# Attention scores issued two head pairs ahead, together with moved modulation sums and split waits, in a two-block transformer kernel

## The reference, cut to what matters

```
first block, DEPTH = 2 layers:
  h = x @ w_in[l]                       # 1024 x 5024, split into latents, gates, q, k, v
  o_a = softmax attention, 8 heads of 96/64 (latents up-projected, rotary on 32 channels)
  o_b = differential attention, 4 heads of 2 x 64
  x = layer_norm(alpha * x + merged(o_a, o_b, gates) @ w_out)

second block, DEPTH = 2 layers:
  mod = silu(c) @ mod_w[i] + mod_b[i]   # 1024 x 9216: shift, scale and gate of three sublayers
  x = half ffn; (layer 0 also: ctx = half ffn)
  layer 0: window attention, 16 query heads, 4 key heads of 64, over 256 banded latent
           keys + 256 context keys + a sink logit per head
  layer 1: fourier mix:  real(fft over tokens of fft over channels, 4 groups of 256) @ fourier_wo
  x = post_norm; x = half ffn
```

## Time and profile before

| | us |
|---|---|
| runs | 1606.33, 1601.07, 1602.33 |
| median | 1602.33 |
| the profiled execution | 1607.04 |
| its span, first to last instruction | 1605.3 |
| TensorE busy in it | 1560.0 (97%) |
| VectorE busy | 1201.6 (75%) |
| ScalarE busy | 795.2 (50%) |
| mean granted TensorE clock | 0.994 |

### The profile page before, as it was taken

One profiled execution on the slowest core, in us unless ns is written; L12 is line 12 of the kernel. 1 busy time (PEld: TensorE's weight loads), 2 busy tenths in 40 slices (PEclk: granted clock), 3 DMA queues, 4 the chain that ended last, 5 costly groups with the idle time before them and its releaser, 6 DMA issues.

```text
span 1605.3 us, 20700 instructions
## 1 busy us (share of the span) xinstructions
PE 1560.0 (97%) x7671; PEld 1289.4 (80%) x7671; DVE 1201.6 (75%) x1853; ACT 795.2 (50%) x1250; POOL 153.7 (10%) x212
## 2 busy tenths in 40 slices
PE   7999998999999999999999899999999999999997
PEld 6888886888788887888877568888888888888886
DVE  7888996898988785877759767877587776575554
ACT  5476543566454453544535656444354443264442
POOL 1100001100011110011100121111011110010000
PEclk9999998999999999999999999999999999999999
DMA  9864558754678876788756217888678874365552
GB/s 343 271 236 146 185 166 288 247 176 143 209 255 271 284 259 216 235 275 278 257 174 207 76 53 254 283 276 277 199 237 277 281 269 164 93 222 184 184 186 77
DMA packets 200652, 349.62 MB, mean 218 GB/s; under 512 B 11204, under 2 KB 128252, under 8 KB 200044
## 3 DMA queue, kind: packets, MB, share of 16 engines
q1 hardware_dynamic: 174812, 252.90, 47.9%
q0 software_dynamic: 25744, 95.43, 16.9%
HBM read 347.21 MB, written 1.08 MB: 217 GB/s over the span
## 4 chain that ended last, share of the span: by engine, by line
PE 84%; DVE 12%; DMA 2%; ACT 1%; issue 1%; SPq 0%; DVEq 0%; POOLq 0%; ACTq 0%
PE acc L618 25%; PE acc L620 24%; PE acc L619 24%; DVE w_lo L1606 2%; PE turn L1008 1%; PE acc L915 1%; PE score L767 1%; DMA mod_raw<-in_mod_w 1%; PE score L895 1%; DVE att_work L2231 1%; DVE acc_ctx L1726 1%; PE score L1106 1%; PE turn L904 1%; DVE wide L1988 1%; PE score L959 1%
## 5 line engine op out<-in xcount | busy, mean ns | idle before, releaser
L1606 DVE TENSOR_TENSOR w_lo<-raw,w_hi 128x1024 fp32r<-128x1024 f32 (+2 forms) x490 | 585.4, 1204 | 245.0 <-ACT w_hi L1222 244.4
L1222 ACT ACTIVATE w_hi<-raw 128x1024 fp32r<-128x1024 f32 (+2 forms) x490 | 502.1, 1039 | 455.9 <-PE acc L620 438.0
L618 PE MATMUL acc<-w_hi,xT_hi 128*128 128x512 f32 (+1 forms) x1440 | 572.1, 397 | 3.5 <-DVE xT_lo L1654 2.1
L620 PE MATMUL acc<-w_hi,xT_lo 128*128 128x512 f32 (+1 forms) x1440 | 561.5, 390 | 0.0
L619 PE MATMUL acc<-w_lo,xT_hi 128*128 128x512 f32 (+1 forms) x1440 | 560.7, 389 | 0.0
L618 PEld LDWEIGHTS acc<-w_hi,xT_hi 128*128 128x128 f32 x1440 | 271.6, 189 | 59.2 <-issue 6.3
L620 PEld LDWEIGHTS acc<-w_hi,xT_lo 128*128 128x128 f32 x1440 | 271.1, 188 | 56.7
L619 PEld LDWEIGHTS acc<-w_lo,xT_hi 128*128 128x128 f32 x1440 | 271.7, 189 | 52.6
L506 POOL DMA_DIRECT2D mod_raw<-in_mod_w x144 | 104.3, 724 | 909.0 <-DVE mod_run L1726 745.4
L618 PE MATMUL acc<-w_hi,hT_hi 128*128 128x512 f32 x440 | 172.8, 393 | 0.0
L620 PE MATMUL acc<-w_hi,hT_lo 128*128 128x512 f32 x440 | 171.4, 390 | 0.0
(11 more groups left out here) (295 smaller groups left out, 1303.6 us busy)
## 6 DMA issues: line engine op xcount, KB each, us to landing
raw<-in_ffn_wi SPq DMA_DIRECT2D x220, 512.0 KB, 5.0
mod_raw<-in_mod_w POOLq DMA_DIRECT2D x144, 512.0 KB, 6.1
raw<-in_ffn_wo SPq DMA_DIRECT2D x110, 512.0 KB, 4.5
raw<-in_w_in SPq DMA_DIRECT2D x72, 512.0 KB, 6.1
raw<-in_w_out SPq DMA_DIRECT2D x16, 512.0 KB, 4.6
raw<-in_attn_wqkv SPq DMA_DIRECT2D x16, 512.0 KB, 4.6
wide<-in_b_merge POOLq DMA_DIRECT2D x4, 1024.0 KB, 9.2
raw<-in_w_branch_a SPq DMA_DIRECT2D x8, 512.0 KB, 4.6
```

What stands on the lines that cost most here:

```text
L618: nc.tensor.matmul(dst, xh, wh, start=start, stop=False)
L620: return nc.tensor.matmul(dst, xl, wh, start=False, stop=stop)
L1222: nc.scalar.activation(piece_part(w_hi[:, i % SPLIT_SLOTS, :], i), piece_part(raw[:, s, i % 2 * PIECE:(i % 2 + 1) * PIECE], i), ACT.Copy). ...
L1606: nc.vector.tensor_tensor(piece_part(w_lo[:, i % RAW_PIECES, :], i), piece_part(raw[:, i // 2 % RAW_SLOTS, i % 2 * PIECE:(i % 2 + 1) * PIE ...
```

## The change

- The second and third modulation sum of layer 1 of the first block go behind the steps n = 1 and n = 3 instead of n = 0 and n = 2. Layer 0 is as it was.
- In the window attention TensorE waits for a new signal, `heads_rotated`, before it turns q, and for the copied keys only before the keys. One of VectorE's splits goes from behind the copy of the keys to the last head pair.
- `scores(u + 2)` is issued inside `turn_probs(u)`: token tile 0 of both heads before the fourth group of turns, token tile 1 behind that group and before the inverse sums. `scores(1)` stays where it was.
- In the fourier stage tile 1 is turned and modulated one group later, behind g = 3 of tile 0 and that group's move and split; the wait for all four banks becomes one wait for each group.

```diff
+        heads_rotated = sem("heads_rotated")
...
                     project(ACC[n % 2 * 2:n % 2 * 2 + 2], 4)
-                    if n % 2 == 0:
+                    if n % 2 == l:
                         mod_sum(True)
...
-                pe.wait_ge(k_twice_ready, 1)
+                pe.wait_ge(heads_rotated, 1)
                 for u in range(4):
                     pairs(u, lambda t, i: qkv[:, t, (2 * u + i) * P:(2 * u + i) * P + P])
...
-                def scores(u):
-                    for t in range(NT):
+                def scores(u, tiles=range(NT)):
+                    for t in tiles:
...
                     for i in range(2):
                         pe.wait_ge(exps_ready, c.next("exps"))
                         for t in range(NT):
+                            if i and t and u + 2 < AH // 2:
+                                scores(u + 2, (0,))
                             b = att_turn(u, 2 * i + t)
...
+                    if u + 2 < AH // 2:
+                        scores(u + 2, (1,))
                     pe.wait_ge(inv_ready, c.next("inv", 2))
...
                 for u in range(AH // 2):
-                    if u + 1 < AH // 2:
-                        scores(u + 1)
+                    if u == 0:
+                        scores(1)
                     if u:
                         values(u - 1)
                     turn_probs(u)
...
-                        if t == 0 and g == FGROUPS - 1:
+                        if t == 1 and g == 0:
                             after.append(turn_tile(1))
...
-                landed(*ACC)
 
                 after = []
                 for g in range(FGROUPS):
+                    landed(ACC[g])
                     b = turn_bank(g)
...
-                    step(nc.vector.tensor_tensor(xs, r0, r1, ALU.add))
+                    return nc.vector.tensor_tensor(xs, r0, r1, ALU.add)
...
-                        rotate_heads(0, 0, AH)
+                        step(rotate_heads(0, 0, AH))
...
-                        rotate_heads(1, 0, AH)
+                        rotate_heads(1, 0, AH).then_inc(heads_rotated, 1)
+                        dve.wait_ge(heads_rotated, 1)
...
-                    rotate_heads(t, AH, ROPED)
+                    step(rotate_heads(t, AH, ROPED))
...
                 m.then_inc(k_twice_ready, 1)
-                split()
...
                     else:
-                        split(2)
+                        split(3)
...
                     for g in range(FGROUPS):
-                        if t == 0 and g == 2:
+                        if t == 1 and g == 0:
                             modulate_tile(1)
```

## The result

Over six runs of each kernel the changed one takes 1607.89 us (median, 1606.53 to 1612.55), the kernel before 1602.55 (1600.56 to 1606.33). The ratio is **1.0032**, 95% interval 1.0020 to 1.0044: some 5 us slower. The forecast was 1603.8, a loss of 1.5, in a range of 1598.0 to 1608.5. The measured time lies in the range, the loss is over three times the forecast one, and it stands on the border of 0.3%, past which "slower" had 0.12.

The account below looks back on a forecast made before the run. TensorE was taken to bound the kernel (busy 97% of the span). Layer 1 +0.7, attention +0.6 and fourier +0.2 sum to +1.5 us on the median 1602.33, giving 1603.8, range 1598.0 to 1608.5.

Parts of the forecast that it names:

- Layer 1's mechanism: Layer 1: the 6.73 us stall isn't removed but goes to pieces 13 and 14, the latter bound by feature 0's load.
- the term +0.3 + 0.4: Layer 1's moved sums: +0.3 us for the stall moving to pieces 13 and 14, +0.4 for the clock.
- I take half, +0.4: Layer 1: half of the 0.9 us loss if the clock returns only after 7.2 us of work, slowing pieces 14 and 15.
- the clock rival: Layer 1: pieces 14, 15 and the second sum run at 1.2 GHz; +8.2 us in total, 1610.5; chance 0.09.
- +0.3: Layer 1: with the second sum moved, it ends at 284.16 against 283.89 before, leaving out the clock.
- The weight load: Layer 1: taken as 0; its rival has SP's weight load delay feature 0, piece 14 3.5 us later: 1607.3, chance 0.07.
- Start of the attention: Attention start: the split taken out brings the first maxima earlier, −0.9 us, between −1.2 and 0.
- the limit named: Attention start: the mask lands at 887.66, while the removed split would bring the first maxima to 887.42.
- The scores: Attention loop: first half fills waits (−0.96, −2.2), values 0 to 5 wait for ScalarE (+4.1): +0.9 us, period 7.17.
- the tail: Attention, last pair: the third split delays the move before the fourth turn by 0 to 1.17 us; +0.6 taken.
- The rival in which ScalarE's move is hidden: Attention: the 4.1 us of waits before values 0 to 5 don't come; −2.6 us in total, 1599.7; chance 0.12.
- Fourier: Fourier stage: tile 1 modulated behind group 3, four groups end at 1370.1 against 1369.94, +0.2 us; bounds −1.7 and +1.2.

Follow-up runs that it names:

- bias_loads_later: The changed kernel with GpSimd's merge-bias and norm-row loads (3 MB) issued one chunk of features later: 1602.16 us, 0.9987 of the kernel before.
- sums_only: The kernel before with only the layer-1 sums moved: 1608.4 us, ratio 1.0028.
- kept_busy_sized: The changed kernel with unread products filling TensorE's waits: 14 before piece 13, 24 before piece 14, 9 before fourier tile 1; 1607.31 us, 1.0019 of the kernel before.
- attention_only: The kernel before with only the attention part of the change: 1605.19 us, ratio 1.0010.
- late_half: The changed kernel with the second half of the scores behind the inverse sums instead of in front: 1605.45 us, 1.0009 of the kernel before.
- fourier_only: The kernel before with only the fourier part of the change: 1604.01 us, ratio 1.0000.
- late_half_bias_later_sums: The kernel before with the attention part, scores' second half behind the inverse sums, bias loads one chunk later and layer-1 sums moved: 1599.93 us, 0.9969.
- attention_late_half: The kernel before with the attention part alone, the second half of the scores behind the inverse sums: 1601.19 us, 0.9980.
- late_half_bias_later: The kernel before with the attention part, scores' second half behind the inverse sums, and bias loads one chunk later: 1599.43 us, 0.9974.
- before_bias_later: The kernel before with GpSimd's merge-bias and norm-row loads issued one chunk later: 1602.97 us, 0.9988.

## Why the prediction was right and wrong

- **Layer 1's mechanism was right.** The stall moved to pieces 13 and 14 and the second part is bound by feature 0's load: the waits are 3.45 and 4.48 us, where 5.10 and up to 5.5 were written. bias_loads_later shows the cause: with the load early the second wait is gone. The fall of the clock was read slightly late, too: 0.84 in the window 264 to 265 puts it at 264.7, 3.7 us after TensorE stopped and not 3.9, which changes nothing in the sum.
- **Its size was wrong: the term +0.3 + 0.4 measured 3.1 in the two profiles and 4.5 in the runs of sums_only.** The step that failed is "I take half, +0.4". It carried the clock's loss over from one fall, piece 13's, and asked if the level would be back in time. It was back (0.90 and 0.95 in the windows from 272 to 276). But behind the next gap, which the forecast had at up to 5.5 us, it was down again, with piece 14 on the path and in two of the three a part of piece 15, in all three unfilled traces with the sum moved; kept_busy_sized puts this at 2.4 us. It is in part what the clock rival said (pieces 14, 15 and the sum at 1.2 GHz), but by another way: the level came back and fell again, it rose within piece 15, and the whole lost 5.3 us and not 8.2.
- **A second fault in the same term: its base.** +0.3 was worked out against one execution, whose old stall ended at 267.69. In the other three traces with the sum in front and the loads as before it ended at 264.0 to 266.2, and the layer was 0.7 to 3.5 us shorter. The profiled execution stood 4.7 us above the median; the forecast said so and still took its stall as typical. Worked from the load instead, the sum would have cost little in front and most of its 1.72 us behind.
- **The weight load does not crowd out the feature's.** The landing is unchanged (63.3 against 63.5 us). The packet by packet turns of the Trainium skill, DMA: Bandwidth & Descriptors (Queues, rings and completion order) gave 0.8 to 3.5 us later; no trace here shows that, though in the changed kernel SP issued two weight loads from 272.1 on, 2.4 us before feature 0 was used. What delayed the load were the 3 MB issued in front of it.
- **Start of the attention: right.** −0.9 forecast, −0.9 measured to the first maxima. In this execution they do not wait for the mask, but the limit named is close: in attention_only TensorE has the scores 1.5 us earlier than before (569.79 against 571.33 from the last sum), but the maxima then wait 0.70 us for the mask.
- **The scores: right in kind.** No wait ahead of turns 1 to 5, and 0.68 us ahead of values 1 to 5 (0.57 ahead of values 0): exact. Pair 0 and the tail came out right too (the last two values +0.45, forecast +0.6). The period is 7.38, not 7.17: half of the scores was priced at 0.96 and takes 1.06 (904.03 to 905.09), twice a period. That makes scores and tail +2.4 where +1.5 was forecast, and the attention +1.5 where +0.6 was. The rival in which ScalarE's move is hidden fails, and late_half shows what would have hidden it. For a longer wait the forecast found no row; before has one, 1.11 us ahead of values 6, where no scores lie in between.
- **Fourier: right without the clock, open with it.** +0.2 forecast, −0.15 in the trace of fourier_only, +1.5 in the changed kernel's. The term priced the 2 us wait at its length alone, as if a wait of 2.09 us couldn't lower the clock.
- **Sum.** That the range held the time is partly its width: layer 1, given +0.7, measured 3 to 4.5. This term, the half's cost in the scores and, in some executions, the clock in the fourier stage turn +1.5 into +5.1 to 5.3. How often the last comes is not known, since only profiled runs show it.

## What to carry to other kernels

A wait on TensorE costs its length and may cost the clock of the work behind it: ask for each new gap what runs next and if that is on the path, and price it apart. Work that sits in a stall bound by a transfer is nearly free there and is paid for when it is moved out; first find what holds the transfer up, here 3 MB of loads that nobody needed yet, issued in front of it. And when a group is moved to fill one wait, ask what its old place was hiding: the same half of the scores, a few lines later, turned a loss of 1.2 us, whose interval just takes in none, into a gain of 2.8.

## What the runs showed of the hardware

The clock's answer to one and the same gap is not fixed. Tile 1's wait of 2.09 us was left unfilled in four traces; the clock fell in after (the 16 products 5.44 us) and late_half (5.37) and stood in fourier_only and bias_loads_later (3.75 each). After the late mask, it fell with 0.70, 0.86 and 0.87 us of waiting (attention_only, kept_busy_sized, late_half_bias_later_sums) and stood with 0.92, 0.77 and 0.65 (bias_loads_later, attention_late_half, late_half_bias_later). In before_bias_later (0.50 at 893 us) and fourier_only (0.50 at 897) it fell in the first pairs with no wait for the mask at all, and in before and sums_only, with the same attention, it did not. The Trainium skill, TensorE: Matmul & The Clock Gate (What's actually happening) says of a kernel's start that the number of slow products differs from run to run of the same kernel; these traces show the like of gaps in the middle. In a forecast such a gap is a chance, not a yes or no. Filled gaps did not let it fall: 1.00 across layer 1 in all three kernels with idle products, at 0.23 us for each such product (24 in 5.52 us).

A group of score products pays at its ends: from the first pair of products to the next are 0.53 us, and from the last to the work behind it 0.53 too (904.03, 904.56, 905.09), where before the pairs inside a full group follow at 0.43 (905.29 to 905.72). Two groups of four products instead of one of eight take 2.12 us a period instead of 1.91, 0.21 more.
